# Input and gate projections as two jobs of seven half-size block products, and the mixers per block from DRAM

## The reference

```python
h = rmsnorm(x, norm_mix_g)
q_a, k_a, v_a, u, q_x = split(h @ w_in, (512, 128, 128, 512, 512))
y_attn = window_attention(q_a, k_a, v_a, sinks)      # chunks of 64, window 128, 8 heads, ALiBi
y_pool = multiscale_pool(u, w_pool, pool_scale)      # mean of 2/4/8/16 tokens minus the token
mem_k, mem_v = split(rmsnorm(mem, norm_mem_g) @ w_mem_kv)      # 256 memory tokens
y_mem = memory_attention(q_x, mem_k, mem_v)          # 4 heads of 128
gates = sigmoid(h @ w_gate + b_gate)                 # three times 1024 columns
merged = sum(gates[i] * (y[i] @ w_branch[i]) for i in (attn, pool, mem))
x = x + merged @ w_out
x = x + square(relu(rmsnorm(x, norm_mlp_g) @ w_up)) @ w_down
out = rmsnorm(x, norm_final_g)
```

## Time and profile before

| | |
|---|---|
| median of three runs | 2760.65 us (2756.08 to 2761.79) |
| the profiled execution | 2761.86 us, its span 2760.2 us |
| PE busy | 2681.4 us, 97% |
| DVE busy | 1616.5 us, 59% |
| ACT busy | 1166.5 us, 42% |
| POOL busy | 535.0 us, 19% |
| DMA | 410.58 MB, 149 GB/s over the span |
| mean granted clock of PE | 0.989 of full speed |

### The profile page before, as it was taken

How to read it: one execution, slowest core, us unless ns; L and a number is a source line. 1 busy time by engine, 2 the same in 40 slices (tenths; PEclk the granted TensorE clock), 3 DMA queues, 4 the chain that set the end, 5 groups by cost and what they waited for, 6 DMA issues and landing times.

```text
span 2760.2 us, 34473 instructions
## 1 busy us (share of the span) xinstructions
PE 2681.4 (97%) x12449; PEld 2213.7 (80%) x12449; DVE 1616.5 (59%) x2253; ACT 1166.5 (42%) x1986; POOL 535.0 (19%) x523
## 2 busy tenths in 40 slices
PE   8999999999999999999699999999999999999998
PEld 7788877887888877888587788878888788888886
DVE  5652347334463326424777865676657768586897
ACT  5542335332443325432545544565445324242433
POOL 3500244012430235012354200000000121121100
PEclk9999999999999999999899999999999999999999
DMA  7323353234533344233678633453335676766752
GB/s 260 134 86 129 107 176 133 90 132 138 180 98 115 114 160 158 84 118 118 221 217 287 194 116 116 158 160 106 115 114 172 153 172 153 179 149 149 199 182 107
DMA packets 320847, 410.58 MB, mean 149 GB/s; under 512 B 13048, under 2 KB 243500, under 8 KB 320684
## 3 DMA queue, kind: packets, MB, share of 16 engines
q1 hardware_dynamic: 293036, 332.99, 37.7%
q0 software_dynamic: 27648, 75.51, 11.1%
HBM read 288.91 MB, written 119.54 MB: 148 GB/s over the span
## 4 chain that ended last, share of the span: by engine, by line
PE 88%; DVE 4%; issue 3%; DMA 3%; SPq 1%; ACT 1%; POOL 0%; DVEq 0%; POOLq 0%; ACTq 0%
PE ps L1557 28%; PE ps L1559 28%; PE ps L1558 28%; PE ps L1562 2%; DMA rows_tm<-in_x 2%; PE ps L1707 1%; DVE s_lo L1211 1%; PE ps L1690 1%; PE ps L1678 1%; DMA piece_f<-mrg_d 0%; PE ps L1651 0%; DMA res_raw<-t_d 0%; SPq L549 0%; SPq L564 0%; DVE u L1271 0%
## 5 line engine op out<-in xcount | busy, mean ns | idle before, releaser
L1557 PE MATMUL ps<-res_hi,s_hi 128*128 128x512 f32 x2016 | 789.5, 392 | 25.8 <-DVE s_lo L1211 16.4
L1559 PE MATMUL ps<-res_hi,s_lo 128*128 128x512 f32 x2016 | 786.6, 390 | 0.0
L1558 PE MATMUL ps<-res_lo,s_hi 128*128 128x512 f32 x2016 | 786.6, 390 | 0.0
L988 DVE TENSOR_TENSOR w_lo<-stage,w_hi 128x2048 fp32r<-128x2048 f32 (+1 forms) x125 | 240.6, 1925 | 456.6 <-ACT w_hi L678 456.5
L1557 PE MATMUL ps<-h_hi,w_hi 128*128 128x512 f32 x1216 | 484.4, 398 | 11.8 <-issue 11.8
L1559 PE MATMUL ps<-h_hi,w_lo 128*128 128x512 f32 x1216 | 475.8, 391 | 0.0
L1558 PE MATMUL ps<-h_lo,w_hi 128*128 128x512 f32 x1216 | 475.6, 391 | 0.0
L1557 PEld LDWEIGHTS ps<-res_hi,s_hi 128*128 128x128 f32 x2016 | 380.1, 189 | 107.4 <-DVE s_lo L1211 16.6
L1559 PEld LDWEIGHTS ps<-res_hi,s_lo 128*128 128x128 f32 x2016 | 379.8, 188 | 79.4
L1558 PEld LDWEIGHTS ps<-res_lo,s_hi 128*128 128x128 f32 x2016 | 380.2, 189 | 78.4
L678 ACT ACTIVATE s_hi<-piece_f 128x512 fp32r<-128x512 f32 x288 | 180.2, 627 | 292.3 <-PE ps L1559 285.9
(11 more groups left out here) (183 smaller groups left out, 3080.0 us busy)
## 6 DMA issues: line engine op xcount, KB each, us to landing
stage<-in_w_gate SPq DMA_DIRECT2D x96, 512.0 KB, 4.5
piece_f<-in_w_up SPq DMA_DIRECT2D x32, 1024.0 KB, 6.4
up_d<-c SPq DMA_DIRECT2D x128, 256.0 KB, 2.4
piece_f<-up_d SPq DMA_DIRECT2D x32, 1024.0 KB, 7.8
stage<-in_w_in SPq DMA_DIRECT2D x60, 512.0 KB, 5.1
rows_d<-c POOLq DMA_DIRECT2D x96, 256.0 KB, 4.9
t_d<-tin POOLq DMA_DIRECT2D x40, 512.0 KB, 3.8
tin<-in_w_down POOLq DMA_DIRECT2D x32, 512.0 KB, 4.4
```

The source lines that it names most:

```text
L988: v.tensor_tensor(w_lo[:, slot, 0:kt, :], stage[:, slot, 0:kt, :], w_hi[:, slot, 0:kt, :].bitcast(F32), ALU.subtract).then_inc(lo_done, 1)
L1557: mm(dst, wh, xh, start=first, stop=False)
L1558: mm(dst, wh, xl, start=False, stop=False)
L1559: return mm(dst, wl, xh, start=False, stop=last)
```

## The change

The 38 output tiles of `w_in` and `w_gate` become quartets of the job scheme. There are two new jobs in front, 0 and 1, of 19 quartets each: the resident matrix is the normed and transposed x of 1024 tokens, and the pieces that stream are 7 of `w_in` and 12 of `w_gate`. All their output tiles are written to a new array `proj_d` in DRAM, the gates' after the tanh. The resident matrix of job 0 is made at the start of the kernel straight on chip (`quarters`, `quarter_sums`); that of job 1 (the second 1024 tokens) and the transposed memory tokens are made in five quartets of job 0 (`NORM_AT`) with the code that the output job used, through `ha_d`, `t_d` and `mt_d`. POOL's sums of `w_out` and `w_down` move into twenty quartets of the two jobs (`SUMS_AT`).

Between the jobs stands a stage `mixers`, written out without a loop. Per block it reads q, k, v, u, the memory queries and the gates back from `proj_d`, and PE weaves attention and memory attention between products of the branches alone. `w_mem_kv` is multiplied there too, in the first two attention steps of block 0. Weights of branches go through a ring of three slots (`w_st`, `w_hi`, `w_lo`), gates through four slots of `temp`. In attention steps 0 and 1 the memory branch of the block before is multiplied, in steps 2 and 3 the pool branch, beside memory attention the attention branch. The first operands of the output job are fetched at the end of the stage (`out_fetch`, `out_rest`).

```diff
-FIRST = [0, 8, 24, 40, 48, 56, 64]
-NQT = 72
+FIRST = [0, 19, 38, 46, 62, 78, 86, 94, 102]
+NQT = 110
+NORM_AT = (1, 4, 7, 10, 13)
+SUMS_AT = tuple(range(2, 12)) + tuple(range(21, 31))
+MIX_FETCH = 34
...
     def piece_of(n):
         j, q = job_of(n), n - FIRST[job_of(n)]
+        if j < 2:
+            return w_inv[:, :, q * PC:(q + 1) * PC] if q < 7 else w_gate[:, :, (q - 7) * PC:(q - 6) * PC]
...
+def step_pieces(b, i):
+    if b == 0 and i < 2:
+        return [("mk", 2 * i), ("mk", 2 * i + 1)]
+    r = 2 if i < 2 else 1
+    return [(r, b - 1 if r == 2 else b, 2 * (i % 2) + z) for z in range(2)]
...
+            def finish(n, which, order):            # ACT, after each output tile
+                if gates(n):
+                    op(tile[:], tile[:], ACT.Tanh, scale=0.5, bias=half_bg[:, m:m + 1]).then_inc(u_rdy, 1)
+                    return
...
+            def mixers():                           # SP
+                sp.wait_ge(prod, ALL_IN)
+                load_u(0)
+                sp.wait_ge(ev_dve, 7 * IN_END)
+                load_weight(2)
+                for k in range(GS):
+                    load_gates(k)
+                sp.wait_ge(s_lo_done, ALL_IN)
+                sp.dma_start(wp_st[:], w_poolv).then_inc(wp_ld, 16)
+                sp.dma_start(q_mem[:], proj_v[:, T_QM:T_QM + 4, columns(0)]).then_inc(qm_ld, 16)
+                for i in range(3, len(WEIGHTS)):
+                    e = WEIGHTS[i]
+                    if e == (2, NBLK - 1, 3):
+                        out_fetch()
+                    load_weight(i)
+                    if e in GATE_AT and GATE_AT[e] >= GS:
+                        load_gates(GATE_AT[e])
...
+            def out_fetch():
+                sp.wait_ge(mv_done, 4 * NBLK)
+                load_slot(OUT_JOB, 0)
+                load_piece(IN_END)
+                load_slot(OUT_JOB, 1)
+                load_slot(OUT_JOB, 2)
+            def out_rest():
+                sp.wait_ge(tile_done, len(RING))
+                for s in range(3, PROD):
+                    if s == 3:
+                        for b in range(4):
+                            sp.wait_ge(*last_of_bank(b))
+                        sp.wait_ge(sum_rdy, len(ADDED))
+                    load_slot(OUT_JOB, s)
+                load_piece(IN_END + 1)
...
+            def mixers():                           # ACT
+                act.wait_ge(mr_ld, 16)
+                act.wait_ge(prod, ALL_IN)
+                op(m_hi[:], m_raw[:], ACT.Copy).then_inc(m_hi_done, 1)
+                hi(0)
+                hi(1)
+                act.wait_ge(wp_ld, 16)
+                op(wp_hi[:], wp_st[:], ACT.Copy).then_inc(wp_hi_done, 1)
...
+            def gated(e, z):                        # DVE; its waits are left out
+                to = resid[b % 2][j][:, z, :] if r == 1 else temp[:, k % GS, z, :]
+                v.scalar_tensor_tensor(out=to, in0=temp[:, k % GS, z, :], scalar=1.0, in1=ring(t),
+                                       op0=ALU.add, op1=ALU.mult).then_inc(bank_of(t), 1)
+            def att_step(b, i):                     # DVE
+                att_max(b, i, 0)
+                if b and i == 0:
+                    y2_low(4 * b - 1)
+                    y1_low(b)
+                if (b, i) == (0, 2):
+                    y1_low(0)
+                att_max(b, i, 1)
...
+                lo(w + 1)
+                att_scale(b, i, 0)
+                att_scale(b, i, 1)
+                gated(pieces[0], 0)
+                gated(pieces[0], 1)
+                lo(w + 2)
+                gated(pieces[1], 0)
+                gated(pieces[1], 1)
+                y0_low(b, i)
...
+            def mixers():                           # PE
+                pe.wait_ge(ev_dve, 7 * IN_END)
+                pe.wait_ge(ev_act, IN_END)
+                pe.wait_ge(pad_rdy, 1)
+                for b in range(NBLK):
+                    values_across(b)
+                    for i in range(TT):
+                        p, q = step_pieces(b, i)
+                        att_scores(b, i)
+                        if b and i == 0:
+                            mem_values(b - 1, 3)
+                        if (b, i) == (0, 2) or b and i == 0:
+                            pools(b)
...
+                            branch(p, 0)
+                            branch(p, 1)
+                            branch(q, 0)
+                            probs_across(b, i)
+                            branch(q, 1)
+                        att_values(b, i)
+                    mem_scores(b, 0)
+                    branch((0, b, 0), 0)
+                    branch((0, b, 0), 1)
+                    mem_across(b, 0)
+                    for j in range(1, 4):
+                        mem_scores(b, j)
+                        branch((0, b, j), 0)
+                        mem_values(b, j - 1)
+                        branch((0, b, j), 1)
+                        mem_across(b, j)
+                mem_values(NBLK - 1, 3)
+                for j in range(4):
+                    for z in range(2):
+                        branch((2, NBLK - 1, j), z)
+
+            jobs(0, IN_END)
+            mixers()
+            jobs(IN_END, NQT)
```

More of the change, by code:

```diff
@@ L30 @@
 NQ = 8
+HALF = NQ // 2
 NKV = 2
@@ L124, in row_slot, with spilled, acted, normed @@
+def spilled(n):
+    return count(spills, n)
+def acted(n):
+    return count(lambda m: gates(m) or squares(m), n)
+def row_quartets(n):
+    return count(adds_rows, n)
+def normed(n):
+    return count(has_norm, n)
+def across(n):
+    return count(hosts, n)
+def summed(n):
+    return count(lambda m: hosts(m) and m != MEM_AT, n)
 def row_slot(n):
-    return n % 2 if n < N_OUT else (n + 1) % 2
+    return 1 if n in NORM_AT else n % 2 if out_job(n) else (n + 1) % 2
 def slot_uses(n):
-    return sum(1 for m in range(n) if adds_rows(m) and row_slot(m) == row_slot(n))
@@ L1548, in _ @@
+            for which in (S1, S3, S2, S4):
+                s_sums(0, which)
+            jobs(0, IN_END)
+            mixers()
+            jobs(IN_END, NQT)
             row_rms(NQT - 1)
```

2197 lines of the change are left out of this document (1158 added, 1039 removed).

## The result

The changed kernel takes 2727.4 us (median of 4 runs, 2726.5 to 2733.7) against 2761.2 of the kernel before: ratio 0.988, 95% interval 0.9864 to 0.9896, 1.2% faster. The forecast was 2686. Its sign was right and the wide range of 2661 to 2738 held the time, but the forecast's own range of 2670 to 2705 did not: the gain is 34 us instead of 75. The profiled execution took 2726.9 us, its span is 2724.7.

What follows compares the result with a forecast made beforehand. PE, busy 97% of the span, was taken to bound the kernel. 103.4 us from 456 fewer products, minus 28 for start, entry and contention beyond the gaps that go, gave 2686.4 against 2761.9; own range 2670 to 2705, 8 in 10 2661 to 2738.

Steps and rivals of the forecast that it cites:

- the landmark: Point where the seventh resident split of the output job ends: 1358.7 us before, forecast at 1283.2.
- part 1: The two new jobs: 456 products fewer give 103.4 us; 38 quartets at 19.04 us, transposes 8.8, one turn 3.
- part 2: Start of the kernel: first product at 36 us, last resident split ends at 58.7, last product of quartet 37 at 777.7.
- part 4: Waits in the mixers: 33 us at the entry, 20 for POOL beside DVE, 4 of half clock; quiet steps cost nothing.
- 33 us in all: Mixers' entry: PE waits 12 us (w_pool), 3 and 3.5 (weights), 10 (pool products); bounds 15 and 45.
- 4 us of half clock: Mixers: after the gaps products come 0.43 us apart instead of 0.23, at 1.2 GHz, costing 4 us.
- I take 20: Mixers: POOL's adds and window sums beside DVE cost 20 us; bounds 0 and 48 (3.4 a step, 14 steps).
- part 5: Way into the output job: piece four starts at +21.7, slots 3 to 6 issued at +33.7, landmark 53.8; bounds 41, 66.
- Serial DVE and POOL: In the mixers, 48 us in place of 20 and 15 more on the window steps, total 2729; chance 0.15.
- Quartets slower than 19.04: New jobs' quartets stretched by POOL's sums and 1 MB of stores: 1.25 us a quartet, 46 us, total 2732; chance 0.08.
- late weights: Branch weights in the mixers take over 9.7 us to land; decides from 12.4, at 13 total 2778; chance 0.07.
- small entry: w_pool lands in time, pool products covered: 20 us for 33 at the mixers' entry, contention 6; 2659; chance 0.14.

Runs made afterwards that it cites:

- c4_all: Changed kernel with a1, c2, a4 and b2 together, and three sums of the first piece ahead of the last quarter sums; 2692.4 us.
- a4: Changed kernel, POOL's second group of weight sums held until the second job's seven resident splits are done, not just its first; 2725.8 us.
- b3: Changed kernel without POOL's sums of the output and down weights and their loads and stores (later values wrong); 2722.9 us.
- e1: Changed kernel with POOL's eight sums of the first two pieces cut to 4 of 512 columns (values wrong); 2720.6 us.
- a1: Changed kernel with the load of `w_pool` issued ahead of the wait for the last product of the jobs; 2724.9 us.
- d2: c4_all with the third weight's high part on ACT and low part on DVE ahead of the first maxima and exponentials; 2694.5 us.
- b1: Changed kernel with POOL's window sums of blocks 1 to 3 replaced by ten tiny memsets (pooled values wrong); 2718.9 us.
- b4: Changed kernel with POOL adding only 16 of 512 columns of each gated product to the sum; 2722.5 us.
- b2: Changed kernel with the next block's window sums behind POOL's first add of the memory steps, so not in attention steps; 2717.7 us.
- c2: As a2, with the last weight's low part and the last four pieces' gated products on DVE ahead of the output job's later low parts; 2721.2 us.
- a2: Changed kernel with the last branch weight issued behind slot 0 and the output job's first piece, ahead of slots 1 and 2; 2726.6 us.
- a5: As a2, with the last weight's low part on DVE ahead of the output job's first low parts; 2730.6 us.
- a3: Changed kernel with the small copies of the attention sinks and their DMA ahead of the first rows of x; 2732.5 us.

## Why the prediction was wrong in size

Right: the 456 products at 0.2267 us; quartets at 19.04; quiet memory steps (9.86 us for 9.8); the rest after the landmark (1402.9 for 1401.5); weights in time. That c4_all has its landmark at 1289.1, near the forecast's 1283.2, doesn't prove the sum: c4_all also saves 10 us of window sums, which the forecast charged in its 20, and 9.9 us on the way out, of which the forecast had charged all but 3. Wrong were the terms of give-back at four places, which came out 6 to 11 us too small each: start 6.1, jobs 10.6, mixers 11.4, way out 10.5.

**The turn, in part 1 ("one turn between jobs, 3").** It cost 10.1. I read the 3 from the up job's turn, in which POOL is idle, and said of POOL's sums only that they fit in a quartet's 19 us. Their average fits; but the unit isn't bound to its quartet, and it fell on the two quartets in which DVE is fullest (50.0 of 60 us busy). a4 took 8 of the 10 away with one wait: 4.6 us are later and longer work on DVE, 2.0 a slower load beside the unit's own transfers, 1.6 half clock. b3 showed 3 us more of the unit's cost in quartets 8 to 12, undivided.

**The start, in part 2 ("The last resident split ends at 58.7").** It ended at 64.8. I laid POOL's and DVE's work side by side, each with its duration alone, in the one stretch where both are busy without a pause. e1 has the end at 57.7 with POOL's sums gone; at least 5.3 of the 7 us are the two engines taking turns. That 57.7 is so near 58.7 is partly luck: the first product came at 39.8 us in e1 (42.9 in the changed kernel) and not at 36, since the quarters ended 3 us later and the small copies of the sinks had no term, and the seven splits behind it were faster than forecast. Part 4 weighed the rule of the Trainium skill for the mixers; it was not applied to the start.

**The entry, in part 4 ("33 us in all", and "4 us of half clock").** The first branch product came at 72.6 us after the last product. The terms give 67 (the first memory product at +6.8, then 31.7 of work and 28.5 of waits), and 71 with the 4 us of half clock. The waits were right: `w_pool` landed when I said (16 for 15), the first memory product came at +6.8, and PE waited 20.8 us for weights and 6.1 and 1.7 for low parts of `y`, where I had 12, 6.5 and 10. The term for half clock was too small: 65 products in four groups behind the waits came at about twice their spacing, 6.8 us in all. a1 gained 4.6, not 9 to 11: the maxima now met the first window sums, and its four tiny operations on two inputs took 0.73 to 0.91 us each, where three of the four take 0.16 in the changed kernel. d2 shows that the rest of the gap has more than one wait in a row. What would shorten it stays open.

**Contention in the mixers, in part 4 ("I take 20").** This size was right by luck: b1 and b4 give about 20. It was spread wrongly. I had "3.4 a step, 14 steps", but POOL has four adds in only six attention steps (the first two of blocks 1 to 3), which makes 20 of the bound of 48, and these steps didn't pay: 14.24 us with the adds and without. A block's one step with window sums takes 5.4 us more and all of its adds 2.2 (b2 got 5.1 us a block back). Beyond the entry the stage missed nearly 10 us of its 11.4: attention steps of 14.24 us for 13.9, which b4 and b1 don't shorten, are about 5 of them, and the rest, block starts among it, I can't divide further.

**The way out, in part 5 ("piece four at +21.7", "landmark 53.8").** Piece four started at +24.3, since its weight was down at +16.1 and not at +13.5, and slot 3 was issued at +36.8 for +33.7. That is 3 us of the miss. The other 7 lie behind that issue: 27.5 us to the landmark for 20.1. The slots had landed by about 1310, but in ACT's order the sixth and seventh split stand behind a split of the second piece, for which it waited 7.1 us; PE had two gaps of 4.4 and 6.2 us, with half clock after each. I had let the seventh split follow the slots alone. No run changed that order. The 9 us that c2 gains by DVE's order are another matter: the forecast had them in it but for the 3.

The rivals. Serial DVE and POOL gave 2729 and the time is 2727, but not by its sum: it had 63 us in the mixers, and these took 20. Its 48 rests on the same 14 steps. Its mechanism is right as the rule says and acts in the turn and at the start as well, where no rival had put it; POOL's work costs at most 38 us in all (8 + 3 + 7 + 20), part of it through loads and half clock, about as much as the entry. Quartets slower than 19.04 didn't come, nor did late weights: with the queue's load raised by 512 KB per weight the slowest landed at 11.6 us, under the break-even of 12.4, and the median is less than half of it. The small entry didn't come: the gap was as long as forecast, and longer with its half clock.

The entry and the way out were inside their bounds; the start and the turn had none. All four misses had one sign: each stage was a sum of durations alone, with one engine followed at a time.

## What to carry to other kernels

Where a change swaps work on the critical engine for new transitions, look at each transition for the two engines that prepare it, and add up their SBUF-to-SBUF work as if they were one engine; in most steady quartets here it cost nothing. Look also at what the helper engine's strict order puts ahead of the split that you follow. Tie the work of a side engine to the stretch in which the others have room, with a wait on the event after the crowded one (a4: one wait, 8 us; b2: two lines moved, 5 us a block). Before the last tile of a stage, order each engine by what frees something for the critical engine, and prepare the next stage after that; moving only one instruction of three moved the wait and gained nothing (a2, a5).

## What the runs showed of the hardware

A POOL add of 4 columns took 0.21 us alone and 2.12 beside a DVE subtraction of 2.28 us with two SBUF inputs; DVE's maximum of 4 columns took 0.16 and 1.38 beside POOL's window sums. Four copies of 4 columns with one input each took 2.67 us beside POOL's sums and 0.48 in a3, which has them 28 us earlier. So the loss doesn't go by the size of the instruction that waits but by that of the other. The Trainium skill, "SBUF — State Buffer", section "Who interferes with whom", has it so: the two engines share a pair of SBUF ports, and whoever issues first holds it for the whole instruction. These traces agree. Four orders of the start ended within 3.1 us of each other (70.4 to 73.5), about the noise of that distance, and the run with POOL's sums cut to 4 columns 7 us earlier (63.8).

After a gap of 5.8 us PE's products came 0.21 us apart instead of 0.12; unused products that cut the gap to 2.2 us kept them at 0.12. Where they left a gap of 3.3 us, products of 512 columns went from 0.23 to 0.43 us apart. The entry changed by 1.1 us, less than the runs tell apart.
